# SSD norm per chunk, sample states and norm spread between the parts of gates 21 to 23, and the S5 branch split per chunk, in a hybrid decoder step

## What is computed

```python
y = y + d * x                                  # SSD output per chunk of 128 tokens
y = y.reshape(bsz, l, A_WIDTH) * jax.nn.silu(z)
return rmsnorm(y, norm_w), new_buf, h          # mean of y*y over 512 channels
...
mixed = gates[:, :, 0] * (y_a @ w_br_a) + gates[:, :, 1] * (y_b @ w_br_b) + gates[:, :, 2] * (y_c @ w_br_c)
x = x + mixed @ w_out
```

## Time and profile before

| what | value |
|---|---|
| median of 3 runs | 1910.81 us (1900.81 to 1911.44) |
| the profiled execution's own time | 1898.15 us |
| its span, first to last instruction | 1896.5 us |
| TensorE busy (share of the span) | 1821.8 us (96%) |
| VectorE, ScalarE, GpSimd busy | 687.3, 377.7, 505.1 us |
| mean granted TensorE clock | 0.98 |

### The profile page before, as it was taken

The page is one execution under the profiler, slowest core; times in us unless marked ns, Lnnn a source line. Parts: engine busy times, 40 slices in busy tenths (PEclk is TensorE's granted clock), DMA queues, the critical chain, the costliest instruction groups (busy, mean ns, idle before and its releaser), DMA issues.

```text
span 1896.5 us, 28609 instructions
## 1 busy us (share of the span) xinstructions
PE 1821.8 (96%) x11549; PEld 1751.6 (92%) x11549; DVE 687.3 (36%) x1402; ACT 377.7 (20%) x913; POOL 505.1 (27%) x483
## 2 busy tenths in 40 slices
PE   6999999999999999899899999999999999999996
PEld 6899899999988888788799999999999999999996
DVE  6836711405423444676764251121111111111125
ACT  5211112242113221443402141100110011001111
POOL 5762112222221111111122232233222322332231
PEclk9999999999999998899999999999999999999998
DMA  5563243232232222433354312233223322342233
GB/s 185 91 134 113 80 140 113 94 89 90 90 115 79 91 79 100 131 119 119 112 193 147 105 62 88 93 118 111 89 88 102 120 89 100 100 134 99 88 118 129
DMA packets 80832, 205.69 MB, mean 108 GB/s; under 512 B 15360, under 2 KB 35072, under 8 KB 80488
## 3 DMA queue, kind: packets, MB, share of 16 engines
q1 hardware_dynamic: 38240, 90.52, 15.1%
q0 software_dynamic: 20912, 72.39, 12.0%
q10 hardware_dynamic: 21592, 41.56, 6.7%
HBM read 179.05 MB, written 24.48 MB: 107 GB/s over the span
## 4 chain that ended last, share of the span: by engine, by line
PE 83%; DVE 6%; issue 4%; POOL 3%; ACT 2%; DMA 2%; ACTq 0%; SPq 0%; DVEq 0%; POOLq 0%
PE ps L1076 25%; PE ps L1077 24%; PE ps L1078 24%; POOL SP L853 1%; POOL WL L828 1%; PE ps L1274 1%; PE ps L1414 1%; PE ps L1277 1%; DVE HL L2055 1%; PE ps L1445 1%; PE ps L1450 1%; DVE X L2063 1%; DMA WH<-in_w 1%; POOL WL L1014 1%; PE ps L1497 1%
## 5 line engine op out<-in xcount | busy, mean ns | idle before, releaser
L1076 PE MATMUL ps<-HL,WH 128*128 128x384 f32 (+1 forms) x2496 | 826.8, 331 | 15.3 <-DVE HL L2055 6.5
L1077 PE MATMUL ps<-HH,WL 128*128 128x384 f32 (+1 forms) x2496 | 812.8, 326 | 0.0
L1078 PE MATMUL ps<-HH,WH 128*128 128x384 f32 (+1 forms) x2496 | 811.0, 325 | 0.0
L1076 PEld LDWEIGHTS ps<-HL,WH 128*128 128x128 f32 x2496 | 474.5, 190 | 28.1 <-issue 15.0
L1077 PEld LDWEIGHTS ps<-HH,WL 128*128 128x128 f32 x2496 | 474.9, 190 | 0.2
L1078 PEld LDWEIGHTS ps<-HH,WH 128*128 128x128 f32 x2496 | 474.3, 190 | 0.0
L828 POOL TENSOR_TENSOR WL<-WRAW,WH 128x1024 fp32r<-128x1024 f32 x136 | 328.1, 2413 | 481.5 <-DMA WH<-in_w 478.5
L825 POOL DMA_DIRECT2D WH<-in_w x136 | 78.8, 579 | 808.4 <-PE ps L1078 796.6
L2055 DVE TENSOR_TENSOR FM<-FS,ps 128x384 f32<-128x384 f32 (+1 forms) x66 | 34.3, 521 | 436.8 <-PE ps L1078 432.8
L1076 PE MATMUL ps<-FL,WH 128*128 128x384 f32 (+1 forms) x528 | 171.4, 325 | 6.6 <-POOL WL L828 6.6
L1078 PE MATMUL ps<-FH,WH 128*128 128x384 f32 (+1 forms) x528 | 170.9, 324 | 0.0
(11 more groups left out here) (316 smaller groups left out, 1674.6 us busy)
## 6 DMA issues: line engine op xcount, KB each, us to landing
WRAW<-in_w SPq DMA_DIRECT2D x145, 512.0 KB, 3.2
WH<-in_w POOLq DMA_DIRECT2D x136, 512.0 KB, 3.6
gate_scratch<-GT ACTq DMA_DIRECT2D x24, 528.0 KB, 3.0
PX<-gate_scratch ACTq DMA_DIRECT2D x24, 528.0 KB, 3.6
X<-in_x ACTq DMA_DIRECT2D x8, 528.0 KB, 4.2
X<-in_x SPq DMA_DIRECT2D x16, 192.0 KB, 4.7
u_scratch<-UF ACTq DMA_DIRECT2D x4, 528.0 KB, 4.4
GF<-gelu_scratch SPq DMA_DIRECT2D x4, 528.0 KB, 5.7
```

The lines of the kernel that those rows point to most:

```text
L1076: nc.tensor.matmul(out, wh, rl, start=start, stop=False)
L1077: nc.tensor.matmul(out, wl, rh, start=False, stop=False)
L1078: return nc.tensor.matmul(out, wh, rh, start=False, stop=stop)
```

## The change

- **Norm.** ScalarE squares y of chunk n-1 in its iteration n (`y_square_act`, in place of the spent z in PX tiles 8 to 11). VectorE adds the four squares up in two instructions (`y_square_sum_dve(n-1)`), between its eviction of y of chunk n and the gating. TensorE sums chunk n-2 at the start of chunk n, behind the first B·C product (`y_sums_pe`). Chunks 7 and 8 are summed behind gate 21's second part. Root, reciprocal and spread lie between parts of gates 21 and 22.
- **Sample states.** Gate 21's first part stands in the middle of the sample chunk's y products. The eight states are made in four pairs between parts of gates 21 and 22, with banks 3 and 6.
- **ScalarE.** Output DMAs, the wait for the norm and both halves of the bias table stand between gate 22's second and third part. Gate 23 is taken in parts, with V's copies, `y_high` of the S5 output in chunks, and `exps(0)` between. The loads of BIASS move behind `pt_rows(0)`.
- **Attention's start.** `scores(1)` and the transposes of V move between gate 23's parts.
- **Branch inputs.** q = 0 (S5) is split per column chunk; of q = 1 one tile is split per step 1 to 4, `y_high` behind `yc_rows(p)`, `y_low` behind `mix(p-1)`. Branch tile 0 waits for each piece.

```diff
@@ TensorE, chunk
             fence_set(cb(0))
+            if n >= 2:
+                y_sums_pe(n - 2)
             for i in range(4):
                 nc.tensor.transpose(bank[3][0:rows, i * P:(i + 1) * P], cols(PX[:, i, :]), IDENT)
...
                 if i == 2:
                     fence_set(last)
+                    if smp:
+                        gate(21, [0])
...
@@ TensorE, between the stages
-        gate(21, [1, 2])
+        gate(21, [1])
+        sample_states([0, 1])
+        y_sums_pe(NBLK - 1)
+        y_sums_pe(NBLK).then_inc(ns_done, 1)
+        gate(21, [2])
+        sample_states([2, 3])
+        y_spread_pe()
+        gate(22, [0])
+        sample_states([4, 5])
+        gate(22, [1])
+        sample_states([6, 7])
+        gate(22, [2])
         pe.wait_ge(h_ok, NBLK + 1 + NSEQ)
-        norm_sum_pe(1)
-        gate(22)
         pe.wait_ge(rs_ok, 3)
         scores(0)
-        gate(23)
-
-
-        pe.wait_ge(ye_ok, NBLK + 1)
+        gate(23, [0])
...
         last.then_inc(vt_mm, 1)
+        gate(23, [1])
+        scores(1)
+        gate(23, [2])
...
@@ the norm's new functions
+    def y_square_sum_dve(j):
+
+        dve, z = nc.vector, PX[:, 8:12, y_cols(j)]
+        dve.wait_ge(pq_done, 3 * KD + j + 1)
+        dve.tensor_tensor(z[:, 0:2], z[:, 0:2], z[:, 2:4], ALU.add).then_inc(pq_used, 1)
+        dve.wait_ge(pq_used, 3 * KD + 2 * j + 1)
+        dve.tensor_tensor(z[:, 0], z[:, 0], z[:, 1], ALU.add).then_inc(pq_used, 1)
+
+    def y_sums_pe(j):
+        w = P if j < NBLK else SMP
+        nc.tensor.wait_ge(pq_used, 3 * KD + 2 * j + 2)
+        return nc.tensor.matmul(bank[4][0:w, 384 + j:385 + j], PX[:, 8, y_cols(j)], prm("ones", 0, 1), start=True, stop=True)
...
@@ ScalarE
-        norm_squares_act(1)
-        gate(21)
-        norm_roots_act(1)
-        outs_landed()
...
+        gate(21, [0])
+        y_square_act(NBLK)
+        gate(21, [1])
+        y_roots_act()
+        gate(21, [2])
+        y_spread_act()
+        gate(22, [0, 1])
+        act.wait_ge(h_ok, NBLK + 1 + NSEQ)
+        out_dma(io["ssd_p"], HS[:, 0, :, :])
+        out_dma(io["ssd_s"], H0[:])
+        act.wait_ge(yn_ok, 4)
         load_bias(1)
-        gate(22)
         load_bias(0)
+        gate(22, [2])
...
+        gate(23, [0])
+        outs_landed()
+        act.wait_ge(vt_mm, 1)
+        for i in range(2):
+            nc.scalar.copy(PX[:, 7, 512 * i:512 * i + 512], bank[6 + i][:]).then_inc(vt_ok, 1)
+        y_high_chunk(0)
+        exps(0)
+        gate(23, [1])
+        y_high_chunk(1)
+        gate(23, [2])
+        y_high_chunk(2)
         pt_rows(0)
...
             if p >= 1:
                 pt_rows(p)
                 yc_rows(p)
+            if 1 <= p <= 4:
+                y_high(1, [p - 1])
...
@@ VectorE
             last.then_inc(ye_ok, 1)
+            if n >= 1:
+                y_square_sum_dve(n - 1)
...
+        y_square_sum_dve(NBLK)
+        new_states([0, 1])
+        y_recip_dve()
+        new_states([2, 3])
+        states_by_sequence(1)
+        new_states([4, 5])
+        y_norm_dve([0, 1])
+        new_states([6, 7])
+        y_norm_dve([2, 3])
...
         maxima(0)
+        y_low_chunk(0)
         probs(0)
         maxima(1)
-        y_low(0)
+        y_low_chunk(1)
+        y_low_chunk(2)
...
-            if p == 1:
-                y_low(1)
-                dve.wait_ge(yh_lo, 8)
             if branch_at(p) is not None and p < NSTEP - 1:
                 mix(branch_at(p))
+            if 1 <= p <= 4:
+                y_low(1, [p - 1])
+            if p == 4:
+                dve.wait_ge(yh_lo, 16)
```

More of the change, by code:

```diff
@@ L430, in build @@
     ]
-    SQ_BASE = [None, 0, 4, 10]
+    SQ_BASE = [None, None, 0, 6]
     LATE = (6, 7)
@@ new lines, in y_recip_dve, with y_spread_at, y_spread_pe @@
+    def y_recip_dve():
+        dve = nc.vector
+        dve.wait_ge(rs_sq, 2)
+        for rows, c0, c1 in ((P, 0, NBLK), (SMP, NBLK, NBLK + 1)):
+            dve.reciprocal(RC[0:rows, c0:c1], RC[0:rows, c0:c1]).then_inc(rc_ok, 1)
+    def y_spread_at(n):
+        return bank[(5, 7, 4)[n]]
+    def y_spread_pe():
+        nc.tensor.wait_ge(rc_ok, 2)
+        nc.tensor.wait_ge(ye_ok, NBLK + 1)
+        for j in range(NBLK + 1):
+            w = P if j < NBLK else SMP
+            last = nc.tensor.matmul(y_spread_at(j // 3)[:, P * (j % 3):P * (j % 3) + w], bc(RC[0:w, j:j + 1], [w, P]),
+                                    IDENT[0:w, 0:w], start=True, stop=True)
+            if j % 3 == 2:
+                last.then_inc(rs_all, 1)
@@ L648, in chunk_spread_pe @@
         last.then_inc(cn_rs, 1)
[L650 to L665, removed]
     def pool_low(q, i):
@@ L1458, in ssd_chunk, with sample_states @@
             last.then_inc(yd_mm, 1)
[L1459 to L1470, removed]
-                                                BTM[:, b % 4, 64 * g:64 * g + 64],
-                                                XD[0:SMP, 256 * g:256 * g + 256], start=True, stop=True)
-                    last.then_inc(ss_mm, 1)
+        def sample_states(bs):
+            for b in bs:
+                if b % 4 == 0:
+                    pe.wait_ge(btm_ok, b // 4 + 1)
+                if b >= 2:
+                    pe.wait_ge(h_ok, NBLK + b)
+                else:
+                    pe.wait_ge(xd_ok, NBLK + 1)
+                for g in range(2):
+                    last = nc.tensor.matmul(bank[(3, 6)[b % 2]][64 * g:64 * g + 64, 0:256],
+                                            BTM[:, b % 4, 64 * g:64 * g + 64],
+                                            XD[0:SMP, 256 * g:256 * g + 256], start=True, stop=True)
+                last.then_inc(ss_mm, 1)
         def scores(p):
@@ L1526, in branch @@
             u = UNIT0["branch"] + t // 2
-            if t % 8 == 0 and chunks[0] == 0:
-                pe.wait_ge(yh_lo, 4 * (q + 1))
+            if t in (8, 16) and chunks[0] == 0:
+                pe.wait_ge(yh_lo, 12 + 4 * q)
             if t % 2 == 0 and chunks[0] == 0:
                 pe.wait_ge(split_ok, u + 1)
-            tile(no, u % 2, 4 * (t % 2), 4, HH, HL, (4, 0, 4)[q], chunks=chunks)
+            ready = (lambda n, k: pe.wait_ge(yh_lo, 4 * n + k + 1)) if t == 0 else None
+            tile(no, u % 2, 4 * (t % 2), 4, HH, HL, (4, 0, 4)[q], before=ready, chunks=chunks)
         def transposed_probs(p):
@@ L1907, in exps, with y_high, y_high_chunk @@
             nc.scalar.activation(SM[:, p % 2, 4, :], SM[:, p % 2, 2, :], ACT.Exp).then_inc(ex_ok, 1)
[L1909 to L1919 removed]
+        def y_high(q, js=range(4)):
+            for j in js:
+                src = PX[:, j, :] if q == 1 else PU[:, 4 + j, :]
+                nc.scalar.copy(HH[:, (4, 0, 4)[q] + j, :], src).then_inc(yh_hi, 1)
+        def y_high_chunk(n):
+            c0, w = CHUNKS[n]
             for j in range(4):
[L1922 to L1923 removed]
+                nc.scalar.copy(HH[:, 4 + j, c0:c0 + w], PU[:, j, c0:c0 + w]).then_inc(yh_hi, 1)
         def load_gate(t):
@@ L1954, in yc_rows @@
             last.then_inc(yc_ok, 1)
-        act.wait_ge(acc_done[2], TILE_END[UNIT0["branch"] - 1])
-        pt_rows(0)
-        y_high(0)
+        gate(23, [0])
[9 more added lines that the diff above has]
+        y_high_chunk(2)
+        pt_rows(0)
+        for r in range(0, P, 16):
+            act.dma_start(BIASS[r:r + 16, :, :],
+                          bass.AP(tensor=bsscr.tensor, offset=0,
+                                  ap=[[P + DSEQ, 16], [4 * BW_S, 2], [1, P + DSEQ]])).then_inc(s_biass, 16)
+        load_gate(0)
+        load_gate(1)
+        exps(1)
         yc_rows(0)
@@ L1964, in _ @@
         act.sem_inc(vn_ok, 1)
-        load_gate(0)
-        load_gate(1)
-        exps(1)
-        y_high(1)
         act.dma_start(KS[:, :, 0:P], io["ks"]).then_inc(s_ks, 16)
```

113 lines of the change are left out of this document (52 added, 61 removed).

## The result

The changed kernel takes 1939.63 us (median of 4 runs, 1933.30 to 1946.21), the kernel before in the same comparison 1906.36 us (1900.81 to 1911.44). The ratio is 1.018, interval 1.0152 to 1.0208: slower by 1.8%. The forecast was 1927, in a range of 1906 to 1944, with a chance of 0.40 for slower by over 1%. As a change, +33.3 us against +16, it is twice what I forecast.

A forecast was written before the change was run, and what follows sets the result against it. TensorE, busy nearly all of the span, was taken as the bound. Terms -7.6, +12.3, +2 (clock), +2 and +7 gave +15.7, about +16: 1914 us for an execution like the profiled one, 1927 beside the median; range 1906 to 1944.

The forecast's parts named there:

- the ring: Attention steps 1 to 4: dealt-out split makes a dependency cycle from pv(p) to pv(p+1), 11.6 us each; +7 us.
- Gates 21 to 23: Chunk 8 to first scores: sample states and norm hidden between gate parts, 33.5 us against 41.1; -7.6 us.
- the sample chunk's border: Start of small sample chunk 8: TensorE's wait for VectorE's adds and the sum, about 2.0 us.
- Chunk borders, the idle: Start of each chunk: TensorE waits 1.5 us for VectorE's adds; with the sums, +12.3 us in all.
- The clock at the borders: Chunk borders: the 1.5 us idle may or may not lower TensorE's clock; taken at +2 us.
- The port: Chunk borders: GpSimd's subtraction could hold off VectorE's new adds, 2.2 us per hit; it just misses, none taken.
- Behind step 5 nothing differs: Attention after step 5: no change in time expected, 0 us.
- Attention's start: First scores to pv(1): ScalarE's order leaves TensorE idle ahead of the first transposed probabilities; +2 us.
- The clock falls at every border: Rival, chunk borders: seven clock falls add +14 to +18 us more, 1942 us; chance 0.15.
- Cover works: Rival, attention's start: probs(0) ready before gate 23 ends, first softmax steps hidden; 1899 us; chance 0.08.
- The ring is slack: Rival, attention steps 1 to 4: the dealt-out split costs 0 and not +7; 1920 us; chance 0.13.
- The port hits: Rival, chunk borders: GpSimd 0.3 us earlier delays VectorE's adds, up to 7 x 2.2 us; 1942 us; chance 0.06.

The follow-up runs named there:

- fill_wait: Changed kernel with seven transposes, their result overwritten later, put ahead of the waiting sum in each chunk; 1919.28 us, ratio 1.0077.
- sum_behind_transposes: Changed kernel with the waiting sum moved behind the chunk's own five transposes; 1922.05 us, ratio 1.0092.
- half_fill: Changed kernel with three transposes, their result overwritten later, put ahead of the waiting sum in each chunk; 1932.47 us, ratio 1.0138.
- port_behind: Changed kernel with GpSimd's subtractions for branch units 2 and 3 held until VectorE's probabilities of steps 3 and 5; 1936.10 us, ratio 1.0187.
- split_whole: Changed kernel with y_high(1) and y_low(1) whole again, ahead of the steps and in step 1; 1920.84 us, ratio 1.0102.
- high_ahead_pt: Changed kernel with ScalarE's y_high(1, [p-1]) moved from behind yc_rows(p) to ahead of pt_rows(p); 1928.85 us, ratio 1.0122.
- later_whole: Changed kernel with each chunk's sum one chunk later and y_high(1), y_low(1) whole again; 1891.22 us, ratio 0.9924.

## Why the forecast was right, and where it was not

**The time: in the range, in part by luck.** For an execution like the profiled one of before I had 1914, and the profiled one of the changed kernel took 1937.2, 23 us more. The 12.7 us that I added for the distance of the median from the profiled execution brought the forecast nearer; in the changed kernel that distance was 2.5. By stretches the forecast is short by 15.5 us in the chunks (27.8 against 12.3), 4.9 in the ring, 2.5 in the step behind it and 4.3 ahead of the change, and too high by 0.9, 1.9 and 1.2 in the others.

**Gates 21 to 23: the waits right, the sum by two errors that meet.** Chunk 8 to the first scores gave -6.5 against -7.6 and +2.0 for the sample chunk's border. Without the border's wait it is -11.1 (53.42 against 64.56): the gates gave 3.5 more than I had, since I counted on 2.4 us of clock there and did not look at the fall at 698.8, and the border cost 4.7 and not 2.0. Clock falls there belong in part to the border: in the changed kernel the one that began at 730.5 lasted 10.2 us.

**Chunk borders, the idle: right.** 7 waits, 1.5 us each, on the instruction named. DVE's chain and its durations held.

**The clock at the borders: this step failed.** I wrote "so 1.5 us idle amid narrow work may go either way: bounds 0 and 7 falls at 1.7 or more (12+). I take +2." It fell at all seven, for 6.8 us in five of them, each a loss of 3.3 and not 1.7. With 27.8 measured less 10.3 for the idle and the sums, the term is +17.5. fill_wait, in which only the idle was filled, gives 17.2 of it back. I had two rows of before, one for and one against (797.23 and 809.60), and took a value near the one against, the price of about one fall. But a border is one pattern that comes again seven times, and the price of a fall had to be taken times the count. A count between none and all does occur: in sum_behind_transposes three of the six borders ahead of chunk 8 fell, for 6.3 us in the chunks. The rival had the term at 14 to 18. So the first scores came at 786.6 and not some 5 us behind 760.9, and the chunk period is 23.9 and not 20.6.

The rule that I weighed there, in the Trainium skill, TensorE: Matmul & The Clock Gate, "Why this matters for your kernels", that gaps up to about 3 us do no harm, does not hold here. Idles of 1.47 us (changed kernel) and 0.99 us (half_fill) came with a fall at every border.

**The port: right at the borders, missed in the ring.** The nine pairs of adds ran undisturbed (0.42 and 0.29 us, the last pair, with fewer columns, 0.23 and 0.19). GpSimd's subtraction, set off by PE's last product of a branch tile and begun when its weights have landed, met the new y_low in two of the four steps, at 2.2 and 2.1 us. I had asked where GpSimd stands against the adds, and not where it stands against the other VectorE instructions that the change brings in. The step "it just misses ... I take none (bounds 0 and 7)" was worked out for one place only. The Trainium skill, SBUF — State Buffer, "Who interferes with whom", says that the instruction that starts first keeps the pair. The trace agrees in both directions: y_low (837.28) began 0.05 us ahead of GpSimd's subtraction and ran its usual 1.26; the subtraction took 3.46 in place of 2.34 to 2.4; and VectorE's next, behind it, was the one held, for 2.2 us. Whoever is delayed first hands the delay back.

**The ring: right, with the port on top.** Four rounds of 11.6 and 1.0 for sample_keys made 47.4; with the port held off it was 48.0 (port_behind), in steps of 11.4, 12.5, 12.3 and 11.8. The two hits make the 52.4, so the term that I sized at +7 was 7.5 and 4.4 of port. The clock added little there: PE's busy time in the ring is 39.2 us against 37.2 before.

**The step after, pv(5) to pv(6): not forecast.** "Behind step 5 nothing differs" is wrong by 2.5 us. The step ran in part at the lower clock that a fall at 873.8 left, and it is 8.95 us in split_whole.

**Attention's start: right within 2.** +0.1 against +2. The chain of ScalarE held within 1.2 us at each point compared; the transposed probabilities came at t = 20.2, 0.7 us earlier than I had them.

**Rivals.** "The clock falls at every border" was right. "Cover works" fell: the idle ahead of the first transposed probabilities is still 3.7 us. "The ring is slack" fell (high_ahead_pt, split_whole). "The port hits" came true for 4.3 us, in another place.

## What to carry to other kernels

When TensorE is made to sum or reduce what another engine has just produced, count back from the consuming instruction in every engine's program: here one chunk more of distance took 30 us off, and the producer's two adds ahead of its own wait ended the wait as well. A short wait in a loop has to be priced with the granted clock behind it, and once per iteration. Idle that a change takes away can give back clock as well, so both sides of the sum need that term. And when an instruction is moved or dealt out on VectorE, ask where GpSimd's long instructions fall against each new place, and not against one.

## What the runs showed of the hardware

An idle of TensorE of 1.0 to 1.5 us in narrow work came, in these loops, with a fall to 1.2 GHz at each of seven iterations, mostly 6.8 us long and worth 3.3 us, twice what the wait itself cost. At 0.6 us there was none. Borders between full chunks with no idle kept the full clock but for one, in later_whole (3.4 us from 642.5). At 0.8 us it was four of seven in one arrangement and none of seven in another with five more transposes ahead of the idle; what tells these two apart stays open. A GpSimd subtraction of 1024 columns that began 0.05 us behind a VectorE subtraction (HL, 1.26 us) took 1.1 us longer itself, and the VectorE instruction of four columns behind took 2.36 us in place of 0.16. Sixteen DMA issues on ScalarE's queue took 8.88 us, 0.56 each, during which its next instruction stood, though its input was ready.
